# Joints between plain pairs and seven-product spans: partial-sum copies, one token sum and two of a layer's sums placed elsewhere in their queues

## The reference, cut to what matters

```python
def swiglu(h, w_gu, w_down):
    g, u = jnp.split(h @ w_gu, 2, axis=-1)
    return (jax.nn.silu(g) * u) @ w_down

for layer in range(2):
    if layer == 1:
        kv = rmsnorm(x, p['kv_norm']) @ p['w_kv']
        ...
    x = x + 0.5 * swiglu(rmsnorm(x, p['ffn1_norm'][layer]), p['ffn1_w_gu'][layer], p['ffn1_w_down'][layer])
    h = rmsnorm(x, p['mix_norm'][layer])
    ...
    x = x + out          # layer 0: Mamba-2 mixer, layer 1: sliding-window attention
    x = x + 0.5 * swiglu(rmsnorm(x, p['ffn2_norm'][layer]), p['ffn2_w_gu'][layer], p['ffn2_w_down'][layer])
y = rmsnorm(x, p['final_norm'])
```

## Time and profile before

| | |
|---|---|
| median of three runs | 2365.61 us (2362.74 to 2367.75) |
| profiled execution | 2369.55 us, span of its instructions 2368.0 us |
| mean granted TensorE clock | 0.986 |
| PE busy | 2273.3 us, 96% of the span |
| VectorE busy | 1721.6 us, 73% |
| ACT busy | 1087.8 us, 46% |
| chain that ended last | PE 77%, VectorE 11%, issue 6%, ACT 3% |

### The profile page before, as it was taken

One profiled execution on the slowest core, in us unless ns is written; L12 is line 12 of the kernel. 1 busy time (PEld: TensorE's weight loads), 2 busy tenths in 40 slices (PEclk: granted clock), 3 DMA queues, 4 the chain that ended last, 5 costly groups with the idle time before them and its releaser, 6 DMA issues.

```text
span 2368.0 us, 46057 instructions
## 1 busy us (share of the span) xinstructions
PE 2273.3 (96%) x17318; PEld 2216.4 (94%) x17318; DVE 1721.6 (73%) x2525; ACT 1087.8 (46%) x1974; POOL 296.1 (13%) x253
## 2 busy tenths in 40 slices
PE   8999999899999999999999899999999899999997
PEld 7999999889888899999999899999988799999997
DVE  7759587878999944858667876785876557678585
ACT  6425253456676623525434443352536535335252
POOL 0000003322222122000000300000052240000004
PEclk9999999999999999999999999999999989999998
DMA  3223232336555422223222222222241122222222
GB/s 128 90 82 105 80 98 89 120 118 188 181 180 180 148 80 80 89 81 98 83 96 89 89 74 87 90 89 89 89 135 36 37 62 80 90 91 87 89 90 93
DMA packets 66257, 235.73 MB, mean 100 GB/s; under 512 B 7889, under 2 KB 8017, under 8 KB 65969
## 3 DMA queue, kind: packets, MB, share of 16 engines
q1 hardware_dynamic: 52560, 187.72, 25.3%
q0 software_dynamic: 8320, 31.52, 4.2%
q10 hardware_dynamic: 5248, 14.76, 2.0%
HBM read 221.31 MB, written 14.64 MB: 100 GB/s over the span
## 4 chain that ended last, share of the span: by engine, by line
PE 77%; DVE 11%; issue 6%; ACT 3%; DMA 1%; POOL 1%; ACTq 0%; SPq 0%; POOLq 0%; DVEq 0%
PE psum L545 33%; PE psum L494 29%; PE psum L512 7%; PE psum L611 3%; DMA wpair<-w 1%; DVE cacc L1931 1%; ACT whi L1073 1%; DVE wlo L1627 1%; PE psum L1007 1%; POOL probs L2490 1%; DVE wlo L1745 1%; DVE grs L2192 1%; DVE rstd L1641 1%; PE psum L765 1%; PE psum L770 1%
## 5 line engine op out<-in xcount | busy, mean ns | idle before, releaser
L1073 ACT ACTIVATE whi<-wpair 128x1024 fp32r<-128x1024 f32 x201 | 212.2, 1056 | 450.6 <-PE psum L494 380.6
L1627 DVE TENSOR_TENSOR wlo<-wpair,whi 128x1024 fp32r<-128x1024 f32 x194 | 241.8, 1246 | 86.7 <-ACT whi L1073 86.5
L494 PE MATMUL psum<-hhi,whi 128*128 128x288 f32 x1232 | 265.1, 296 | 0.4
L494 PE MATMUL psum<-hlo,whi 128*128 128x288 f32 x1232 | 264.8, 296 | 0.0
L494 PE MATMUL psum<-hhi,wlo 128*128 128x288 f32 x1232 | 264.8, 296 | 0.0
L1858 DVE SCALAR_TENSOR_TENSOR up<-psum,rstd 128x576 f32<-128x576 f32 x96 | 72.7, 757 | 224.5 <-PE psum L494 210.7
L2387 POOL TENSOR_TENSOR sqsum<-x 128x576 f32<-128x576 f32 x6 | 10.5, 1758 | 1553.6 <-DVE x L1861 1503.7
L494 PEld LDWEIGHTS psum<-hhi,whi 128*128 128x128 f32 x1232 | 198.1, 189 | 1.2 <-issue 1.2
L494 PEld LDWEIGHTS psum<-hhi,wlo 128*128 128x128 f32 x1232 | 198.1, 189 | 0.0
L494 PEld LDWEIGHTS psum<-hlo,whi 128*128 128x128 f32 x1232 | 198.1, 189 | 0.0
L545 PE MATMUL psum<-Thi,qhi 128*128 128x288 f32 x592 | 175.4, 296 | 9.0 <-DVE wlo L1745 4.7
(11 more groups left out here) (342 smaller groups left out, 6434.1 us busy)
## 6 DMA issues: line engine op xcount, KB each, us to landing
wpair<-w SPq DMA_DIRECT2D x349, 512.0 KB, 3.6
seg<-decay_rows ACTq DMA_DIRECT2D x16, 576.0 KB, 4.0
h0s<-ssm_state POOLq DMA_DIRECT2D x16, 512.0 KB, 5.8
h0T<-ssm_state_t POOLq DMA_DIRECT2D x16, 512.0 KB, 3.9
ssm_s<-h0s POOLq DMA_DIRECT2D x16, 512.0 KB, 3.5
E<-decay_rows ACTq DMA_DIRECT2D x32, 144.0 KB, 4.1
x<-x_in SPq DMA_DIRECT2D x8, 288.0 KB, 6.6
y<-ybuf SPq DMA_DIRECT2D x8, 288.0 KB, 2.4
```

What stands on the lines that cost most here:

```text
L494: last = pe.matmul(acc[:, 2 * pair + half, 0:HALF], wt[s][:, k * P:(k + 1) * P], m[:, k0 + k, half * HALF:(half + 1) * HALF], start=start ...
L1073: act.activation(whi[n % 2][:], wraw[n % 2][:], ACT.Copy).then_inc(weights_hi, counts)
L1627: dve.tensor_tensor(wlo[n % 2][:], wraw[n % 2][:], whi[n % 2][:].bitcast(F32), ALU.subtract).then_inc(weights_lo, counts)
```

## The change

Four things are moved; no instruction is added or dropped. In the first pair of every span (twelve) ACT copies the first partial sum ahead of S3 and A12, and the third ahead of the next pair's S1. In the first span of each block (four) the `hhi` copy of the last plain pair goes behind that first copy, and VectorE's `hlo` of it goes from ahead of S3's low part to behind the next pair's weight sums. In block 0 token slice 1 goes from ahead of the norm to behind the first hidden values. In block 2 slices 2 and 3 go from `key_value` into the two plain pairs, and slices 0 and 1 get their `Thi` and `Tlo` one kv unit later.

```diff
-TURNS = {0: {0: (0, 0), 1: (0, 0), 2: (1, 1), 3: (1, 2)}, 1: {0: (0, 1), 1: (0, 2), 2: (1, 1), 3: (1, 2)},
-         2: {}, 3: {0: (0, 1), 1: (0, 2), 2: (1, 1), 3: (1, 2)}}
+TURNS = {0: {0: (0, 0), 1: (0, 2), 2: (1, 1), 3: (1, 2)}, 1: {0: (0, 1), 1: (0, 2), 2: (1, 1), 3: (1, 2)},
+         2: {2: (0, 1), 3: (0, 2)}, 3: {0: (0, 1), 1: (0, 2), 2: (1, 1), 3: (1, 2)}}
...
-                        act.wait_ge(evicted, m + 2 * i + 4)
-                    act.activation(hhi[:, i, :], hidden[:], ACT.Copy).then_inc(h_hi, 1)
+                        if not last:
+                            act.wait_ge(evicted, m + 2 * i + 4)
+                    if not last:
+                        act.activation(hhi[:, i, :], hidden[:], ACT.Copy).then_inc(h_hi, 1)
...
-                if not first:
+                if first:
+                    act.wait_ge(prod, 6 * q + 1)
+                    act.activation(part[:, 0, :], b1, ACT.Copy).then_inc(kept, 1)
+                    if c.a == 0:
+                        act.wait_ge(evicted, c.m + 2)
+                        act.activation(hhi[:, PLAIN[c.ph] - 1, :], hidden[:], ACT.Copy).then_inc(h_hi, 1)
+                else:
                     act.wait_ge(prod, 6 * q)
                 quad_hi(c, S3, s)
...
                 if not first:
                     act.wait_ge(combined, 4 * q - 1)
-                act.wait_ge(prod, 6 * q + 1)
-                act.activation(part[:, 0, :], b1, ACT.Copy).then_inc(kept, 1)
+                    act.wait_ge(prod, 6 * q + 1)
+                    act.activation(part[:, 0, :], b1, ACT.Copy).then_inc(kept, 1)
...
-                    act.wait_ge(summed_w, 3 * q + 6)
-                    quad_hi(c, S1, 1 - s)
+                    if not first:
+                        act.wait_ge(summed_w, 3 * q + 6)
+                        quad_hi(c, S1, 1 - s)
                 act.wait_ge(prod, 6 * q + 3)
                 act.activation(part[:, 2, :], b1, ACT.Copy).then_inc(kept, 1)
                 if not last:
+                    if first:
+                        act.wait_ge(summed_w, 3 * q + 6)
+                        quad_hi(c, S1, 1 - s)
                     quad_hi(c, S2, 1 - s)
...
                     split_hi(n + c + 2, 0)
-                    kv_turned_hi(c)
-                    if c < 2:
-                        gained_whole(2, gain, c + 2)
+                    if c in (1, 2):
+                        kv_turned_hi(c - 1)
...
                     gained(k, gain)
+                gained_whole(2, gain, 2)
+                gained_whole(2, gain, 3)
...
-                hidden_lo(v, PLAIN[ph] - 1)
...
                     sums(c, q + 1, 1 - s, at + 1)
+                    if first and c.a == 0:
+                        hidden_lo(c.v, PLAIN[c.ph] - 1)
...
                     split_lo(n + c + 2, 0)
-                    turn_one(2, c)
-                    if c:
-                        turned_lo(2, c - 1)
-                turned_lo(2, 3)
+                    if c < 2:
+                        turn_one(2, c)
+                    elif c < 4:
+                        turned_lo(2, c - 2)
```

## The result

The changed kernel took 2350.95 us (median of five runs, 2348.66 to 2356.15) against 2367.75 us (2362.74 to 2370.65) for the kernel before beside it: ratio 0.9924, interval 0.9909 to 0.9940. That is faster, by 16.8 us between the medians (18.0 by the ratio), where 12.8 had been forecast; the time lies in the forecast range of 2346 to 2359. Run once more later, beside 11 runs of before, the same program gave 0.9939 (0.9925 to 0.9954), or 14.5 us by the ratio (15.0 between the medians). The profiled execution of the first series has a span of 2347.1 us, 20.9 less than before.

What follows compares the result with a forecast made beforehand. TensorE (PE) was taken as the path, so only its idle time could be won. Joints 8.0 (3.2 + 7.0 - 2.2), opening 0, keys and values 4.8: 12.8 us off 2365.61 gives 2352.8 us, range 2346 to 2359.

Steps and rivals of the forecast that it cites:

- First joints: Four joints, one per layer: 1.70 us stall removed, VectorE's addition limits the gain to 0.8 us each, 3.2 us.
- Other joints: Eight joints: 1.02 us of stall each, VectorE's room allows 0.87 each, remaining wait 0.15; 7.0 us.
- Late weights: Second pair of four joints: VectorE's waits for weights take back 2.2 us, ends 0 and 4.4.
- Half: Late weights: half of about 1.1 us taken as lost at each of four joints, 0.55 x 4 = 2.2 us.
- Opening: Layer zero: PE leaves its wait 1.65 us earlier but starts pair three at 56.46 as before; net 0.
- the rival in its strongest form: Rival 2, opening pays too: 1.65 us earlier start plus 3.1 us of half clock, 2348.1 us; chance 0.10.
- Keys and values: Ahead of layer three: PE's wait falls from 9.41 to 4.6 us, 4.8 us won.
- The clock term: After the wait ahead of layer three: 1.9 us lost to half clock stays, with +1.2 as dear end.
- Layer three's pairs: Layer three's plain pairs: the two moved token sums fit VectorE's idle stretches of 4.51, 3.36 and 1.24 us; cost 0.
- the third piece of work: Layer three's plain pairs: a Tlo of 1.3 us, 0.1 over its idle stretch, counted as 0.
- own sign of being wrong: Forecast wrong if PE waits on S1 or token sums at layer three's first span, or partial sums two and three hold PE.
- The ends listed for the range: Late weights ±2.2, opening +0.5 and -1.5, clock -1.2, first joints -0.6, some 2 us scatter: 2346 to 2359.

Runs made afterwards that it cites:

- hlo_ahead: The changed kernel with hlo back in its old place ahead of S3's low part on VectorE; 2355.06 us, ratio to before 0.9937.
- room: Changed kernel with hlo back ahead of S3's low part, plus S4's low part behind VectorE's addition into part; 2347.81 us, ratio to before 0.9919.
- joints_only: Kernel before with only the edits at the twelve joints, without those of TURNS and key_value; 2359.56 us, ratio 0.9962.
- changed_third: The changed kernel unaltered, run for a third trace; single time 2354.46 us.
- kv_late: Changed kernel with slice one's low part put off behind the eight xlo, into layer three's first plain pair; 2354.1 us, ratio to before 0.9934.
- code_shift: The changed kernel with 128 increments of an unused semaphore ahead of PE's first matmul; 2363.18 us, ratio to before 0.9968.
- open_late: The changed kernel with layer zero's second to fourth token sums each put off; 2353.69 us, ratio to before 0.9933.

## Why the prediction was right

**First joints: right.** Forecast 0.8 us each and a new wait of 0.9 on the addition; measured 0.80, 0.80, 0.73 and 0.95 us, and a wait of 0.72, worth 0.87 with the 0.15 of overlap. The addition is 0.54 us later (82.47 for 81.93), forecast 0.52. `hlo_ahead` shows that the `hlo` move is what costs it. One term is right by luck: the 0.15 us taken for the hand-over from VectorE to PE. PE starts 0.06 us after the addition (82.92, then 82.98), but the product behind it then starts 1.70 us later instead of 1.60, and the two make about 0.15 together.

**Other joints: right.** Forecast 0.87 each; 0.84 or 0.85 at seven of eight in the first trace, the eighth being the next point. That VectorE's addition is the limit is shown by `room`: moved forward by 0.6 us, it gave another 0.35 at each. The 1.2 us that `room` wins there are also more than the 1.02 that the prediction counted as stall: behind each of the two stalls the next product started 0.08 us late as well. It did no harm, since the room and not the stall set the forecast.

**Late weights: this step failed.** I took 2.2 us off. The three traces of the changed kernel lost 0.4, 0.0 and 0.3 us at the eight other joints against the 6.83 of `joints_only`. Two things were wrong in the term. Four waits of 1.1 us (1.04 to 1.47 each in the trace of before) don't come back in each program: at the joints the first trace of the changed kernel had one of 1.04, at 321.99, and two of 0.5 or less. And the delay has to pass the room that VectorE has gained by the second pair. Its additions into `part` are 10.5 us apart (178.72, then 189.21) and PE's pairs 11.1, so there is 0.65 us. At the joint of the late load the additions are 11.5 us apart (319.50, then 331.00), and PE runs 0.05 us behind the second of them:

```profile
189.21 0.45 DVE L1820 TENSOR_TENSOR part<-psum,part 128x288 f32<-128x288 f32 x1
...
319.50 0.45 DVE L1820 TENSOR_TENSOR part<-psum,part 128x288 f32<-128x288 f32 x1
...
331.00 0.45 DVE L1820 TENSOR_TENSOR part<-psum,part 128x288 f32<-128x288 f32 x1
```

```profile
331.50 0.40 PE L545 MATMUL psum<-Thi,qhi 128*128 128x288 f32 x1
```

The delay of 1.04 cost 0.36, the smaller ones nothing. Later traces bear this out: waits of 0.82 and 0.91 (`changed_third`), 0.96 (`kv_late`) and 1.07 us (`hlo_ahead`) cost 0.11, 0.21, 0.27 and 0.36. "Half" stood for a number that could be read. The cause itself, an instruction packet beside the load, is now shown by `code_shift`. The rule of the Trainium skill (Runtime: NRT & Kernel Launch, Instruction fetch mechanics), that fetch is hidden, would have made the sum 15.0, nearer to what came; but the traces don't bear it out for the neighbours: the loads are slowed, VectorE's room hides a delay only up to 0.65 us, and `room` lost 1.25 us to one by way of ACT.

**Opening: right.** Forecast: PE leaves at 26.4 and starts pair three at 56.46. Measured 26.39 and 56.39. The first trace even refutes the rival in its strongest form. After the shorter wait the granted clock was full, by stretch, length, busy us of the engines and clock:

```profile
26.39:39.41 13.02, 13.02 (x96) 12.78 (x96) 10.36 (x10) 7.21 (x9) 0.00 (x0) 1.00 0.27 81
```

PE was 4.4 us ahead of before at the end of this stretch and lost it all at 41.73, 49.39 and 56.39, waiting for VectorE. That a full clock can bring nothing there is shown; `open_late` shows what does. The net of 0 is the kinder reading, though. From the first matmul to the first span the seven traces in which this is the opening's one change took 60.9 to 61.1 us, the four with the old opening 61.0 in the first trace of before, which had 6.8 us at half clock, and 60.5 to 60.7 in the three others, which had 3.4. So the move wins nothing and may lose some 0.3 us.

**Keys and values: right.** Forecast 4.6 us of wait and 4.8 won; 4.56 and 4.85. The clock term had 0 with 1.2 as the dear end: 0.3 to 0.7 us were lost there against the first trace of before, 0.7 to 1.1 against the second.

**Layer three's pairs: nearly.** I set the third piece of work to 0 because the span's first product needs no token sum. The second one does, and the `Tlo` stands ahead of S1's low part:

```profile
1378.01 1.35 DVE L1693 TENSOR_TENSOR Tlo<-Tf,Thi 128x1152 fp32r<-128x1152 f32 x1
1379.28 0.69 DVE L1757 TENSOR_TENSOR wlo<-wsum,whi 128x512 fp32r<-128x512 f32 x1
```

S1 x T1 starts 1.68 to 1.76 us after the first product in the first two traces instead of 1.60, so layer three's first joint won 0.73 and 0.58, not 0.81 (in the second trace another late load, a wait of 0.77 us, took the last 0.08). The raw weights of the last plain pair were late by 0.57 and 0.65 us just before; in `kv_late`, where VectorE waited 0.34 us for them, the start is at 1.61 again. By the prediction's own sign of being wrong, a wait on S1 in this span, this step was off, by some 0.1 us.

**The sum.** 12.8 forecast; 14.2 from the edits in the trace, the difference being the late weights (+1.8) less the clock behind the kv wait (-0.3). The 20.9 between the profiled executions hold 6.7 us that no edit touches, most of it half clock in attention; the second trace of before shows that this comes without the edits. That the 16.8 of the first series hold some of the same is likely, as the second series gave 14.5, but only one execution of that series was traced. The ends listed for the range add up to 2348.1 and 2360.3 and not to 2346 and 2359; 2350.95 lies inside either way.

## What to carry to other kernels

When a copy is moved forward to free PE, look for the next thing that PE takes from the engine that did not move: its room, not the stall, is what can be won, and moving that engine's one late instruction (here S4's low part behind the addition) then brings the rest. Put off work that nobody awaits, but look for what it now stands in front of: the `Tlo` ahead of S1's low part took back 0.1 us in one place and 0.7 in another. And where totals scatter by more than the edit is worth, time the same two instructions in both traces, stage by stage, and take a second trace of the unchanged kernel before a difference in an untouched stage is put down to the edit.

## What was not expected of the hardware

- Instruction packets slow the weight loads that they meet: 3.5 us becomes 4.0 in the median and up to 6.5, and lengthening one engine's code moves the place.
- The half clock in stages with short waits differs from execution to execution of one program: attention 234.8 or 240.1 us, the mixer 419.6 to 422.7 in the changed kernel with 6.8 to 17.1 us at half clock. What decides it was not tried.
- The last down projection of each block runs at one of two rates with the granted clock full throughout. Stretch, length, PE busy, clock, DMA share and GB/s for 243 matmuls, before and then changed:

```profile
1291.30:1323.30 32.00, 32.00 (x243) 1.00 0.39 115
```

```profile
1285.78:1317.18 31.40, 31.40 (x243) 1.00 0.38 117
```

  From the start of one matmul to the next it is 133.5 or 130.7 ns on average, in either kernel, and 0.8 us hang on it each time. Its cause stays open.
